# Two index chunks without rows 0 to 63: rounded and low parts of rows 64 to 127 in one stationary operand, the two chunks in turn, the row-major input loaded later

## The reference

```python
h = rms_norm(x, norm_gain)                       # rstd per row, then gain per column
proj = h @ w_in                                  # 2048 x 13,392 columns
qa, ka, va, ga, qi, ki, wi, qb, kb, vb, gb, ma, mb = split(proj)
qa, ka, qb, kb = rope(rms_norm(...))             # heads of 128
qi, ki = rope(qi), rope(ki)                      # indexer: 16 query heads x 64, one key of 64
score = sum_h relu(qi_h . ki) * wi_h             # causal; top 64 keys per row are selected
oa = softmax over the selected keys              # branch A, 8 heads
ob = softmax_0 - lam * softmax_1, then a norm    # branch B, 4 heads of two maps
merged = sigmoid(ma) * ((oa * silu(ga)) @ w_o_a) + sigmoid(mb) * ((ob * silu(gb)) @ w_o_b)
return x + merged @ w_out
```

## Time and profile before

| | |
|---|---|
| median of three runs | 785.3 us |
| the profiled execution | 785.47 us, its span 783.7 us |
| TensorE busy | 779.6 us (99%), 3,672 products |
| VectorE, ScalarE, GpSimd busy | 502.2 (64%), 419.7 (54%), 98.2 us (13%) |
| DMA | 171.0 MB, mean 218 GB/s, over 300 GB/s in the first 39 us |
| chain that ended last, whole span | TensorE 97% |
| granted TensorE clock | full (1.00) in every slice |

### The profile page before, as it was taken

How to read it: one execution, slowest core, us unless ns; L and a number is a source line. 1 busy time by engine, 2 the same in 40 slices (tenths; PEclk the granted TensorE clock), 3 DMA queues, 4 the chain that set the end, 5 groups by cost and what they waited for, 6 DMA issues and landing times.

```text
span 783.7 us, 10539 instructions
## 1 busy us (share of the span) xinstructions
PE 779.6 (99%) x3672; PEld 656.1 (84%) x3672; DVE 502.2 (64%) x695; ACT 419.7 (54%) x675; POOL 98.2 (13%) x160
## 2 busy tenths in 40 slices
PE   9999999999999999999999999999999999999998
PEld 9998888888888888888888888888888888888887
DVE  6787777777777655568646456565655567764553
ACT  7674476666654555556455554555476434444331
POOL 4442422222221000000000003001010011100000
PEclk9999999999999999999999999999999999999999
DMA  9988878898888775666655667866785878775553
GB/s 310 321 260 275 256 217 237 250 265 247 240 238 235 203 202 164 190 188 186 188 153 168 167 176 229 221 199 191 202 228 193 294 221 252 238 224 190 195 192 122
DMA packets 86938, 171.00 MB, mean 218 GB/s; under 512 B 6576, under 2 KB 14576, under 8 KB 86640
## 3 DMA queue, kind: packets, MB, share of 16 engines
q1 hardware_dynamic: 80752, 152.06, 64.5%
q0 software_dynamic: 5856, 18.09, 8.4%
q10 hardware_dynamic: 288, 0.30, 0.1%
HBM read 159.29 MB, written 11.14 MB: 217 GB/s over the span
## 4 chain that ended last, share of the span: by engine, by line
PE 97%; ACT 1%; DMA 1%; issue 0%; SPq 0%; DVE 0%; ACTq 0%
PE ps L644 30%; PE ps L646 30%; PE ps L645 30%; PE ps L655 3%; DMA raw<-in_w_in 1%; PE ps L733 0%; PE ps L834 0%; PE ps L833 0%; PE ps L832 0%; PE ps L741 0%; ACT L1034 0%; ACT L926 0%; ACT g L926 0%; PE ps L721 0%; ACT hi L913 0%; PE ps L749 0%
## 5 line engine op out<-in xcount | busy, mean ns | idle before, releaser
L1164 DVE TENSOR_TENSOR lo<-raw,hi 128x1024 fp32r<-128x1024 f32 (+2 forms) x279 | 334.5, 1203 | 251.8 <-ACT hi L913 250.9
L913 ACT ACTIVATE hi<-raw 128x1024 fp32r<-128x1024 f32 (+2 forms) x277 | 287.5, 1040 | 319.0 <-PE ps L646 284.2
L644 PE MATMUL ps<-hi,hT_hi 128*128 128x512 f32 (+2 forms) x936 | 362.8, 388 | 0.0
L645 PE MATMUL ps<-lo,hT_hi 128*128 128x512 f32 (+2 forms) x936 | 360.8, 385 | 0.0
L646 PE MATMUL ps<-hi,hT_lo 128*128 128x512 f32 (+2 forms) x936 | 360.8, 385 | 0.0
L646 PEld LDWEIGHTS ps<-hi,hT_lo 128*128 128x128 f32 x936 | 175.7, 188 | 34.9
L644 PEld LDWEIGHTS ps<-hi,hT_hi 128*128 128x128 f32 x936 | 175.8, 188 | 33.4
L645 PEld LDWEIGHTS ps<-lo,hT_hi 128*128 128x128 f32 x936 | 175.8, 188 | 32.9
L644 PE MATMUL ps<-hi,ogT_hi 128*128 128x512 f32 x128 | 49.8, 389 | 0.0
L645 PE MATMUL ps<-lo,ogT_hi 128*128 128x512 f32 x128 | 49.8, 389 | 0.0
L646 PE MATMUL ps<-hi,ogT_lo 128*128 128x512 f32 x128 | 49.8, 389 | 0.0
(11 more groups left out here) (178 smaller groups left out, 537.8 us busy)
## 6 DMA issues: line engine op xcount, KB each, us to landing
raw<-in_w_in SPq DMA_DIRECT2D x192, 512.0 KB, 4.3
raw<-in_w_out SPq DMA_DIRECT2D x32, 512.0 KB, 3.7
raw<-in_w_o_a SPq DMA_DIRECT2D x16, 512.0 KB, 6.3
raw<-in_w_o_b SPq DMA_DIRECT2D x16, 512.0 KB, 4.5
turned<-swapped POOLq DMA_DIRECT2D x11, 512.0 KB, 3.3
raw<-in_w_in SPq DMA_DIRECT2D x13, 384.0 KB, 5.2
v<-turned POOLq DMA_DIRECT2D x32, 128.0 KB, 6.2
raw<-in_w_in SPq DMA_DIRECT2D x8, 336.0 KB, 4.9
```

What stands on the lines that cost most here:

```text
L644: mm(o, a_hi, w_hi[:, j], start=first and j == 0, stop=False)
L645: mm(o, a_hi, w_lo[:, j], start=False, stop=False)
L913: activation(hi[:, slot, :, 0:width], raw[:, slot, :, 0:width], ACT.Copy).then_inc(hi_ready, 1)
L1164: tt(lo[:, slot, :, 0:width], raw[:, slot, :, 0:width], hi[:, slot, :, 0:width].bitcast(F32), ALU.subtract).then_inc(lo_ready, 1)
```

## The change

- The first 16 units take chunks 0 and 1 in turn: (0,0), (1,0), (0,1), (1,1), and so on, all 16 with `early_unit`.
- Chunks 0 and 1 are computed for rows 64 to 255 alone. Row tile 1 has its three products. Row tile 0 has two: the stationary operand `packed_rows(k)` is 64 columns of the rest of x for rows 64 to 127 and 64 columns of the rounded x for the same rows, times the weights' hi and lo. PSUM rows 0 to 63 then hold rest x weights, rows 64 to 127 rounded x weights. `hT_lo` gets 320 columns per k tile in place of 256 for it, and ScalarE writes the rounded x of rows 64 to 127 there once more (`x_hi_again`, 64 columns per k tile).
- The results: ScalarE copies PSUM rows 0 to 63 of row tile 0 to `swapped[64:128]`, and VectorE adds it to `stage[64:128]` before the rope.
- Chunk 2 has all rows and three products as before; it collects in banks 6 and 7 and waits for no other chunk.
- Moved, in positions (c, i): sines from ahead of block 11 to ahead of block 16; chunk results to (1,7), (2,3), (3,0); ropes to (2,0) to (2,2), (2,4) to (2,6), (3,1) to (3,3); squares of `x_own` to (3,1), (3,4); the quarters of `x_own` behind (2,1), (2,3), (2,5), (2,7); the index key's rope and transposes to (4,6), scaled by the row norm there; on GpSimd the full tables ahead of the root, the third index chunk's way to DRAM and all three chunks' way back to the second of the eight rounds, their readers one chunk later.
- `ident` and `ki_hi` share space with other tensors. Later uses of `hT_lo` only take the new addresses.

The core of the diff:

```diff
@@ -48,7 +48,8 @@
 EARLY = 3
-X_OWN_AFTER = ((1, 3), (1, 5), (1, 7), (2, 1))
+X_OWN_AFTER = ((2, 1), (2, 3), (2, 5), (2, 7))
+LO_STEP, LO_W = P + P // 2, P + P // 2 + P
 CK = 8
@@ -93,8 +94,10 @@
-FIRST_UNITS = ((0, 0), (1, 0), (0, 1), (1, 1)) + tuple((c, i) for c in range(2) for i in range(2, CK))
-FIRST_END = CK + 2
+PACKED = 2
+FIRST_UNITS = tuple((c, i) for i in range(CK) for c in range(PACKED))
+FIRST_END = 2 * CK - 1
 assert IDX_W[0] == IDX_W[1]
@@ -110,6 +113,9 @@
 INDEX_CHUNKS = (C_INDEX, C_INDEX + 2)
+INDEX_OUT = ((1, 7), (2, 3), (3, 0))
+INDEX_ROPE = (2 * CK, 2 * CK + 4, 3 * CK + 1)
@@ -131,7 +137,7 @@
-    return 2 * ((c + 1) % 2)
+    return 6 if c == PACKED else 2 * ((c + 1) % 2)
@@ -162,7 +168,16 @@
         hT_hi = sb("hT_hi", [P, KT, S], F32R)
-        hT_lo = sb("hT_lo", [P, KT, S], F32R)
+        hT_lo_flat = sb("hT_lo", [P, KT * LO_W + P // 2], F32R)
+        hT_lo = hT_lo_flat[:, 0:KT * LO_W].rearrange("p (k n) -> p k n", n=LO_W)
+        def lo_rows(k, r):
+            return hT_lo[:, k, r * LO_STEP:r * LO_STEP + P]
+        def packed_rows(k):
+            return hT_lo[:, k, P // 2:P // 2 + P]
@@ -241,7 +255,7 @@
-        index_turned = [three_blocks(at) for at in (16, 19, 24)]
+        index_turned = [three_blocks(at) for at in (16, 19, 12)]
         index_landing = [three_blocks(at) for at in (32, 35, 27)]
@@ -566,14 +578,21 @@
             ts(sub_gain[:, :], sub_gain[:, :], 1.0 - LAMBDA_INIT, None, ALU.mult).then_inc(tables_ready, 1)
-            for n in range(C_QK):
-                pool.wait_ge(index_turns, n + 1)
-                pool.dma_start(index_home[n], index_turned[n]).then_inc(index_kept[n], 16)
+            pool.wait_ge(x_squares, RT)
+            root(rstd, ms_x, ss_x, D, RT, NORM_EPS).then_inc(rstd_ready, 1)
+            def keep_index(t):
+                pool.wait_ge(index_turns, t + 1)
+                pool.dma_start(index_home[t], index_turned[t]).then_inc(index_kept[t], 16)
+            keep_index(0)
+            keep_index(1)
             for n in range(8):
                 root(r_h, ms_h, ss_h, HD, 8, NORM_EPS).then_inc(r_h_ready, 1)
-                for t in range(C_QK if n == 0 else 0):
+                if n == 1:
+                    keep_index(2)
+                for t in range(C_QK if n == 1 else 0):
                     pool.wait_ge(index_kept[t], 16)
@@ -650,29 +669,33 @@
-                def products(stationary, moving, j, first=False, last=False):
-                    for r in range(RT):
-                        ins = mm(ps[:, chunk_bank(c) + r, 0:IDX_W[0]], stationary[:, 2 * unit_k + j, r * P:(r + 1) * P],
-                                 moving[:, u % RING, j, 0:IDX_W[0]], start=first, stop=last)
-                    return ins
+                bank = chunk_bank(c)
+                o_0, o_1 = ps[:, bank, 0:IDX_W[0]], ps[:, bank + 1, 0:IDX_W[0]]
                 for j in range(2):
+                    k, w_hi = 2 * unit_k + j, hi[:, u % RING, j, 0:IDX_W[0]]
+                    first = unit_k == 0 and j == 0
                     pe.wait_ge(hi_first if j == 0 and u < EARLY else hi_ready, u + 1)
                     pe.wait_ge(x_hi_first if j == 0 and u == 0 else split_hi, unit_k + 1)
-                    products(hT_hi, hi, j, first=unit_k == 0 and j == 0)
+                    mm(o_1, hT_hi[:, k, P:S], w_hi, start=first, stop=False)
                     pe.wait_ge(x_lo_first if j == 0 and u == 0 else split_lo, unit_k + 1)
-                    products(hT_lo, hi, j)
+                    mm(o_1, lo_rows(k, 1), w_hi, start=False, stop=False)
+                    if j == 0 and u == 0:
+                        pe.wait_ge(x_again_first, 1)
+                    mm(o_0, packed_rows(k), w_hi, start=first, stop=False)
                 for j in range(2):
+                    k, w_lo = 2 * unit_k + j, lo[:, u % RING, j, 0:IDX_W[0]]
+                    last = unit_k == CK - 1 and j == 1
                     pe.wait_ge(lo_first if j == 0 and u == 0 else lo_ready, u + 1)
-                    ins = products(hT_hi, lo, j, last=unit_k == CK - 1 and j == 1)
+                    mm(o_1, hT_hi[:, k, P:S], w_lo, start=False, stop=last)
+                    ins = mm(o_0, packed_rows(k), w_lo, start=False, stop=last)
                 ins.then_inc(unit_done, 1)
...
                 if not isinstance(c, int) or c >= 2:
-                    if i == 0:
+                    if i == 0 and not (isinstance(c, int) and c == PACKED):
                         pe.wait_ge(chunk_out, c - 1)
-                    unit(c * CK + i, i % RING, 2 * i, hT_hi, hT_lo, bank, i == 0, i == CK - 1, width)
+                    unit(c * CK + i, i % RING, 2 * i, hT_hi, lo_rows, bank, i == 0, i == CK - 1, width)
@@ -888,8 +909,12 @@
                 for k in (2 * t, 2 * t + 1):
+                    x_hi_again(k)
                     ins = activation(hT_hi[:, k, :], x_tile(k), ACT.Copy, scale=gainT[:, k:k + 1])
                 ins.then_inc(split_hi, 1)
+            def x_hi_again(k):
+                return activation(hT_lo[:, k, P:LO_STEP], x_tile(k)[:, P // 2:P], ACT.Copy, scale=gainT[:, k:k + 1])
@@ -921,14 +946,15 @@
                 act.wait_ge(unit_done, chunk_end(c))
+                if isinstance(c, int) and c < PACKED:
+                    activation(swapped[P // 2:P, 0, 0:width], ps[0:P // 2, bank, 0:width], func)
                 for r in range(RT):
...
                     for r in range(RT):
-                        ins = activation(kst[:, r, :], ps[:, bank + r, width:width + KIWI], func,
-                                         scale=rstd[:, r:r + 1])
+                        ins = activation(kst[:, r, :], ps[:, bank + r, width:width + KIWI], func)
                 ins.then_inc(chunk_out, 1)
@@ -980,7 +1006,9 @@
             act.wait_ge(x_landed[0], 16)
+            x_hi_again(0).then_inc(x_again_first, 1)
             act.wait_ge(x_landed[1], 16)
+            x_hi_again(1)
             activation(hT_hi[:, 1, :], x_tile(1), ACT.Copy, scale=gainT[:, 1:2]).then_inc(split_hi, 1)
@@ -991,30 +1019,24 @@
                     make_hi(u, u % RING, u // RING, IDX_W[0])
-            for i in range(FIRST_END - RING, CK):
-                if i == CK - 1:
-                    act.wait_ge(reduced, 1)
-                    activation(sin_t, ang, ACT.Sin).then_inc(sin_ready, 1)
-                    activation(cos_t, absr, ACT.Sin, scale=-1.0, bias=HALF_PI).then_inc(sin_ready, 1)
-                make_hi_ahead(0, i)
             for c in range(1, C_QK + 2):
-                for i in range(CK):
-                    if c == 2 and i in (2, 4):
-                        r = (i - 2) // 2
+                for i in range(FIRST_END - RING - CK if c == 1 else 0, CK):
+                    if (c, i) == (1, 4):
+                        act.wait_ge(reduced, 1)
+                        activation(sin_t, ang, ACT.Sin).then_inc(sin_ready, 1)
+                        activation(cos_t, absr, ACT.Sin, scale=-1.0, bias=HALF_PI).then_inc(sin_ready, 1)
+                    if c == C_QK and i in (1, 4):
+                        r = i // 4
                         act.wait_ge(x_own_landed[r], 2 * 16)
-                        junk = qkT[:, 8 * r:8 * (r + 1), :].rearrange("p a b -> p (a b)")
-                        ins = activation(junk, x_own[:, r, :], ACT.Square, accum_out=ss_x[:, r:r + 1])
-                        if r == RT - 1:
-                            ins.then_inc(x_squares, 1)
-                    if c == 1 and i == 2:
-                        index_chunk(0)
-                    if (c, i) == (3, 0):
+                        act.wait_ge(x_squares, r)
+                        junk = qkT[:, 0:8, :].rearrange("p a b -> p (a b)")
+                        activation(junk, x_own[:, r, :], ACT.Square, accum_out=ss_x[:, r:r + 1]).then_inc(x_squares, 1)
+                    if (c, i) in INDEX_OUT:
+                        index_chunk(INDEX_OUT.index((c, i)))
+                    if (c, i) == (C_QK + 1, 0):
                         act.wait_ge(rstd_ready, 1)
-                    if c >= 2 and i == 0:
-                        if c <= C_QK:
-                            index_chunk(c - 1)
-                        else:
-                            qk_chunk(c - 1, chunk_bank(c - 1))
+                    if c > C_QK and i == 0:
+                        qk_chunk(c - 1, chunk_bank(c - 1))
                     make_hi_ahead(c, i)
@@ -1022,7 +1044,7 @@
                         qkT_out(c - 2)
-                    if c == C_QK + 2 and 3 <= i <= 5:
+                    if c == C_QK + 3 and 3 <= i <= 5:
                         index_T_out(i - 3)
@@ -1209,40 +1232,51 @@
                     dve.wait_ge(chunk_out, n + 1)
+                    if n < PACKED:
+                        upper = stage[P // 2:P, 0, 0:IDX_BLOCKS[n] * P]
+                        mark(tt(upper, upper, swapped[P // 2:P, 0, 0:IDX_BLOCKS[n] * P], ALU.add))
+                        settle()
```

(76 more changed lines are left out.)

44 lines of the change are left out of this document (26 added, 18 removed).

## The result

The changed kernel took 790.41 us (median of 6 runs, 789.29 to 791.15) against 785.02 us of the kernel before (6 runs beside it, 784.72 to 785.6): a ratio of 1.0066, 95% interval 1.0055 to 1.0076. It is slower by 5.4 us. The forecast was 785.0, "no change", in a range of 781.6 to 788.0; the time lies 2.4 us above the range. The median of the six runs lies 1.1 us above the profiled one, which is the fastest of them; only that one left a trace, and the 1.1 us stay unexplained.

What follows compares the result with a forecast made beforehand. TensorE, never idle, was taken as the bound: 5.36 us ahead at unit 16, less 0.4 sine block, 4.4 stalls in chunk 2 and 0.1 own input, left 0.5 off 785.47, so 785.0 us; range 781.6 to 788.0.

Steps and rivals of the forecast that it cites:

- The saving: Units of chunks 0 and 1: one of six products per k tile goes, 5.55 us; 5.36 ahead at unit 16.
- The ring: First 16 units: four weight blocks go round in 6.6 us against TensorE's 6.93, landing 4.75; no stall before unit 16.
- the sine block: Moved between hi of 15 and hi of 16: TensorE stalls 0.4 us at unit 16, bounds 0 and 1.3.
- Unit 20: Chunk 2: TensorE stalls some 1.3 us, with 2.5 us of first rope and added sum ahead of lo 20.
- Unit 24: Chunk 2: TensorE stalls some 3.0 us, of 4.4 in the chunk, waiting for lo behind the second rope.
- GpSimd beside it: Second rope and lo 24 meet GpSimd's full tables: 0.35 us more on seven instructions, 2.5 us, bounds 0 and 7.9.
- own input: Four loads moved to units 17 to 23: landing 5.3 to 5.8 us, 0.1 slack taken at unit 19, then hidden.
- B: Rival: second rope and lo 24 lose 0.8 us on each of seven instructions to GpSimd's tables, 5.6; 788.1 us, chance 0.17.
- A: Rival: landing 4.3 us, slack survives, no stall at unit 16, GpSimd meets half the rope; 782.0 us, chance 0.35.
- C: Rival: packed product isn't cheaper, TensorE keeps its pace and the extra work stays; 786.0 us, chance 0.05.

Runs made afterwards that it cites:

- T and O: Changed kernel with own input loaded in chunk 3 and either GpSimd's tables after the second rope, 782.36 us, or second and third ropes in chunk 3, 782.43 us.

## Why the prediction failed

**The saving, right.** 160 products at a step of 0.173, 5.52 us ahead at unit 16 (forecast 5.36). From unit 1 to unit 16 are 26.47 us where 150 steps are 26.00, so 0.47 is lost there (forecast 0.2), most of it at the first products of unit 2; but unit 1 starts 0.79 us earlier than before, 0.44 more than its two missing products, and that pays for it.

**The ring, right in the first stage.** Landing 4.5 us (4.75). The stall of 0.4 from the sine block didn't come, unit 16 started without a wait.

**Unit 20, right.** 1.37 us against 1.3, the added sum 0.60 with its wait against 0.47, the rope 2.6 against 2.5. The slack at unit 19 was 0.3 us (lo 19 ends at 38.93, the unit starts at 39.26) against 0.1.

**Unit 24, wrong: "GpSimd beside it", 2.5 us, and "the second rope starts 7.5 us after lo 19".** The wait was 5.90 instead of 3.0. From lo 19's end to lo 24's end I had 11.2 + 2.5 = 13.7 us; it took 55.70 - 38.93 = 16.8. Of the 3.1 more, 1.5 is contention: 4.0 us on eight instructions, 0.50 each, where I had 0.35 on seven. The 0.35 came from the lo blocks of the earlier trace rows, a mean over a stretch. The other row that I had weighed, two small rope products that met the tables, gave 0.5 each and 3.5 us for seven, and it was the nearer one: the same kind of instruction, wholly beside GpSimd. The trace of before had the answer for lo too, in the spread of the same five blocks (shortest, median and longest in ns):

```profile
L1164 DVE TENSOR_TENSOR lo<-raw,hi x5: 1226/1690/1759, 50.9 to 58.1; 128x1024 fp32r<-128x1024 f32 x5
```

In the order of their starts they took 1.23, 1.69, 1.76, 1.76 and 1.42: three lost 0.47 to 0.54 us against 1.217. The first, at 50.85, started 0.1 us ahead of GpSimd's first product (50.94) and lost nothing, and that product took 1.74 us instead of the 0.74 of one alone. The mean of 1.571 hid both. Another 1.4 is lateness of lo 23, 8.9 instead of 7.5 us after lo 19, since own input put the landing at 6 to 7.2 us where I had 5.3 to 5.8 and called it hidden; ScalarE's copies of chunk 1 ahead of block 23 then had no slack to lie in. The rest, 0.2, is rounding of the rope's and lo's own length.

**The clock, missing.** There was no term for it. A wait of 5.9 us took TensorE to 1.2 GHz and cost 1.7 us by the profile, 2.3 by the medians of the run with TensorE kept busy.

**Sum.** Forecast 785.0, profiled 789.3: contention 1.5, late blocks 1.4, clock 1.7, less 0.4 for the sine block, is 4.2 of the 4.3. Against the median of 790.4 another 1.1 us is open.

**The rivals.** B had the place and the sign right (chunk 3 after 55.6 us, 55.84 measured), and its price of 0.8 per instruction was too high (0.5 on eight instead of 0.8 on seven); it came near its time, 788.1, because lateness and the clock added what the price didn't. So the place was foreseen and the closeness of the number is partly luck. I had ranked it third for the wrong reason, the 0.35. The Trainium skill, "SBUF — State Buffer" (SBUF: two separate sides), says of a VectorE instruction with two SBUF inputs and a GpSimd instruction that reads SBUF that whichever starts first holds the shared ports for the whole instruction while the other is blocked. The traces agree with that: the lo that started first lost nothing, and each instruction that started behind one of GpSimd's lost 0.42 to 0.53 us, while that one had 0.56 to 0.66 still to run. What doesn't come out is my reading of it in the prediction, a whole instruction of 1.13 us for each: what is lost is about the rest of the one under way. A and C are refuted for this kernel. A's 782.0 is near what the kernel gives with T and O out of the way (782.36 and 782.43), but by another road than a landing of 4.3 us and half of the rope met. The section of the Trainium skill cited for A, "DMA: Bandwidth & Descriptors" (Anatomy of one DMA), is written for transfers that GpSimd issues, and these loads are SyncE's; by the estimate of 2.9 us they would all have been faster than measured: no run's median for 384 KB is below 4.2.

**What each part costs**, by the medians: tables away 4.3, own input away 1.7, both 8.0 (790.41 - 782.36), more than their sum. At unit 24 itself the two simply add: moving the tables takes 4.0 us off the wait with the own input in place (5.90 to 1.92) and 4.1 with it away (4.66 to 0.58). What doesn't add lies elsewhere: with the own input alone away the clock still falls, and with the tables alone away there are 1.4 us of small waits that the kernel with both later nearly lacks. Keeping TensorE busy 2.3. Not tried: another place for the first rope, whose wait of 0.6 to 1.0 us at unit 20 stays in the two best versions. Left open: the small waits behind 80 us.

## What to carry to other kernels

When a change makes the leading engine faster in one stage, write down the slack of the next stage in microseconds first; here it fell from 3 us (ahead of unit 15 before) to 0.3 (ahead of unit 19 after), and everything that had been free in it (a rope, a 2 MB load, tables on GpSimd) got a price at once. Price a conflict of two engines from instructions of which the trace shows that they lay wholly beside each other, not from a mean over a stretch; shortest, median and longest of the group show at once whether the mean is a mixture. Where the sum contains a wait of several microseconds on TensorE, add a term for the clock behind it.

## What the runs showed of the hardware

The clock. After a wait of 5.9 us TensorE ran eight products of 512 columns at 0.427 us each before it was back at 0.227, after 4.7 us eleven, after 3.3 and 4.1 us eight; waits of 1.92 and 1.98 us left the clock at 1.00. After the wait of 4.1 us the first three products still ran at full speed and the eight at half speed came behind them, so the price falls on work that looks blameless. The Trainium skill, "TensorE: Matmul & The Clock Gate" (Part 1: The HAM clock gate), names the same two levels and puts the lower one to an idle array; the granted clock of 0.50 in the stretches agrees.

The conflict of VectorE and GpSimd slows the one that starts second. GpSimd's 256-column product took 0.74 us where VectorE left it alone and up to 1.78 beside it, in the kernel with own input and tables later:

```profile
53.03 0.74 POOL L582 TENSOR_TENSOR g<-v 128x256 f32<-128x256 f32 x1 [17.88 <-DVE qkT L1261]
53.73 1.78 POOL L584 TENSOR_TENSOR g<-v 128x256 f32<-128x256 f32 x1
```

The second of these products started 0.05 us behind a lo of VectorE (53.68), which took its usual 1.23 us; the next lo started within it and took 1.54. TensorE hardly waited there (0.2 us ahead of one unit, at 64 us): the same conflict, starting 3 us behind the start of unit 24 instead of 8 us ahead of it, costs next to nothing.
